# A hybrid decoder layer on one core: the output projection moved between the recurrence's steps, attention outputs with tokens as rows, and the low-rank work inside the first key slabs

## The reference, cut to what matters

```python
proj = x @ w_in[l]
y_rwkv = _rwkv7_mixer(proj[..., :RWKV_COLS], ...)
y_diff = _diff_attention(proj[..., RWKV_COLS:], ...)
mix = jnp.concatenate([y_rwkv, y_diff], axis=-1) @ w_out[l]
x = _layer_norm(DEEPNORM_ALPHA * x + mix, ln1_gain[l], ln1_bias[l])
h = jnp.square(jax.nn.relu(x @ w_ff1[l])) @ w_ff2[l]
x = _layer_norm(DEEPNORM_ALPHA * x + h, ln2_gain[l], ln2_bias[l])
...
# in the mixer: decay and a from low-rank products, kk = k * k_k normalised by head
w = -jax.nn.softplus(-(w0 + jnp.tanh(w_d) @ w_up)) - 0.5
a = jax.nn.sigmoid(a0 + a_d @ a_up);  g = jax.nn.sigmoid(g_d) @ g_up
y = (y - mean) * rsqrt(var + eps) * gn_gain + gn_bias;  out = (y + bonus) * g
...
# in the attention, for each head of 128 values
out = out * lax.rsqrt(jnp.square(out).mean(-1, keepdims=True) + SUBLN_EPS) * subln_gain
out = out * (1.0 - lambda_init)
```

## Time and profile before

| what | value |
|---|---|
| median of 3 runs | 1323.35 us (1322.83 to 1326.43) |
| the profiled execution | 1328.44 us, of which the span is 1326.7 us |
| PE busy | 1273.9 us (96%) |
| DVE, ACT, POOL busy | 738.2, 567.2, 82.3 us |
| mean granted TensorE clock | 0.986 |
| bytes read | 218.83 MB, 167 GB/s over the span |

### The profile page before, as it was taken

How to read it: one execution, slowest core, us unless ns; L and a number is a source line. 1 busy time by engine, 2 the same in 40 slices (tenths; PEclk the granted TensorE clock), 3 DMA queues, 4 the chain that set the end, 5 groups by cost and what they waited for, 6 DMA issues and landing times.

```text
span 1326.7 us, 24389 instructions
## 1 busy us (share of the span) xinstructions
PE 1273.9 (96%) x10200; PEld 1096.8 (83%) x10200; DVE 738.2 (56%) x762; ACT 567.2 (43%) x615; POOL 82.3 (6%) x53
## 2 busy tenths in 40 slices
PE   6999999999999889989999999999999999999995
PEld 6899999999777767877888888888888888888884
DVE  4367766363575135677555555555555555655557
ACT  4643444445554123454333333333344444444443
POOL 0021112000000010029200000000000000000000
PEclk9999999999999899999999999999999999999998
DMA  8254565223300234564555555555565555555541
GB/s 325 101 195 163 187 221 192 96 101 101 126 32 5 109 148 145 197 229 146 193 179 183 188 188 190 189 184 179 183 252 192 192 191 194 196 197 188 194 160 64
DMA packets 33671, 222.02 MB, mean 167 GB/s; under 512 B 4773, under 2 KB 5157, under 8 KB 7742
## 3 DMA queue, kind: packets, MB, share of 16 engines
q1 hardware_dynamic: 33598, 220.94, 47.2%
HBM read 218.83 MB, written 2.10 MB: 167 GB/s over the span
## 4 chain that ended last, share of the span: by engine, by line
PE 90%; DVE 5%; ACT 3%; issue 2%; DMA 0%; SPq 0%; DVEq 0%; ACTq 0%
PE ps L447 89%; DVE wlo L1362 1%; DVE x1f L1736 0%; DMA stage<-w_in 0%; ACT whi L1054 0%; DVE stats L1701 0%; DVE xres L1806 0%; PE ps L707 0%; DVE xres L1700 0%; DVE xres L1804 0%; ACT L1054 0%; DVE acts L1750 0%; ACT xres L1054 0%; ACT kr L1054 0%; DVE yt L1659 0%
## 5 line engine op out<-in xcount | busy, mean ns | idle before, releaser
L1362 DVE TENSOR_TENSOR wlo<-stage,whi 128x2048 fp32r<-128x2048 f32 x192 | 447.9, 2333 | 429.4 <-ACT whi L1054 428.3
L447 PE MATMUL ps<-acts,whi 128*128 128x256 f32 (+1 forms) x2400 | 622.8, 337 | 16.7 <-DVE wlo L1362 14.8
L1054 ACT ACTIVATE whi<-stage 128x2048 fp32r<-128x2048 f32 x194 | 371.8, 1917 | 593.5 <-PE ps L447 590.5
L447 PE MATMUL ps<-acts,wlo 128*128 128x256 f32 x1712 | 483.8, 283 | 0.5 <-issue 0.5
L447 PEld LDWEIGHTS ps<-acts,whi 128*128 128x128 f32 x2400 | 409.5, 191 | 72.9 <-issue 20.8
L447 PEld LDWEIGHTS ps<-acts,wlo 128*128 128x128 f32 x1712 | 327.2, 191 | 0.7 <-issue 0.7
L447 PE MATMUL ps<-whi,shi 128*128 128x512 f32 x632 | 249.5, 395 | 2.8 <-DVE slo L1673 2.7
L447 PE MATMUL ps<-wlo,shi 128*128 128x512 f32 x632 | 248.0, 392 | 0.0
L447 PE MATMUL ps<-whi,slo 128*128 128x512 f32 x632 | 247.8, 392 | 0.0
L447 PEld LDWEIGHTS ps<-whi,shi 128*128 128x128 f32 x632 | 119.5, 189 | 35.7 <-issue 6.8
L447 PEld LDWEIGHTS ps<-wlo,shi 128*128 128x128 f32 x632 | 119.5, 189 | 25.4
(11 more groups left out here) (206 smaller groups left out, 839.4 us busy)
## 6 DMA issues: line engine op xcount, KB each, us to landing
stage<-w_ff SPq DMA_DIRECT2D x128, 1024.0 KB, 4.9
stage<-w_in SPq DMA_DIRECT2D x51, 1024.0 KB, 4.9
stage<-w_out SPq DMA_DIRECT2D x16, 1024.0 KB, 4.9
xstage<-xT SPq DMA_DIRECT2D x4, 512.0 KB, 7.0
xres<-x SPq DMA_DIRECT2D x1, 2048.0 KB, 7.8
gain<-ln_gain SPq DMA_DIRECT2D x2, 1024.0 KB, 8.0
bias<-ln_bias SPq DMA_DIRECT2D x2, 1024.0 KB, 10.1
out<-xres SPq DMA_DIRECT2D x8, 256.0 KB, 2.2
```

Of the source, the lines that this page charges most:

```text
L447: return pe.matmul(out, lhsT, rhs, start=start, stop=stop, skip_group_check=True)
L1054: return act.activation(out, in_, func, **kw)
L1362: TTn(wlo[k0 % NHL][:, :], stage[k0 % NST][:, :], f(whi[k0 % NHL][:, :]), ALU.subtract).then_inc(s_lo, 1)
```

## The change

Six things are edited. (1) 18 products of a zeroed tile (`WARM`) stand ahead of slab 0, and slabs 0 to 2 are loaded and split in halves, with their columns in one layout of 384. (2) The low-rank block is cut into pieces that stand inside slabs 4 to 7 (`low_rank`); the sines move to chunks 6 to 8. (3) `bonus_and_kk(j - 1)` moves from c = 0 to c = 1, and the roots for it to c = 0; the triangular solves start one slab later. (4) The attention outputs are computed with tokens as rows, four heads at a time; the squares are summed by DVE, and PE transposes the normalised result (`heads_turned`). (5) The output projection goes by quarters of the columns (`out_rows`), and its first six slabs stand in pieces between the recurrence's steps and the group norm's; `w_out` is loaded earlier; the gate is copied out of PSUM by ACT. (6) The last slabs go by token tile, and the layer norm's additions by quarter, with `scales(0, 0)` behind the last of them.

```diff
+WARM = 18
...
-        FIRST_SLAB = (1, 8)
+        FIRST_SLAB = (2, 9)
...
+        def out_bank(a, q):
+            return (6, 4, 2, 0)[q] + a
...
+            def low_rank(g, part):
+
+                at_half = 2 * (g - G_MIX) + part
+                if at_half == 2:
+                    pe.wait_ge(s_cst, 16)
+                    pe.wait_ge(s_lup, 32)
+                    pe.wait_ge(s_lora, 1)
+                    pe.wait_ge(s_vec, 1)
+                    pe.wait_ge(s_free, 2)
+                    for a in range(TT_):
+                        for q in range(2):
+                            mm(ps[:, 4 + 2 * a + q, :], wt[:, tok(a)], wup[:, 512 * q:512 * q + 512]).then_inc(s_z, 1)
+                items = {3: range(0, 4), 4: range(4, 8), 5: (8, 9), 6: (10, 11), 7: (12, 13), 8: (14, 15)}
+                for n in items.get(at_half, ()):
+                    b, bk = n % NB, 4 + n % 4
+                    if n < 4:
+                        pe.wait_ge(s_sig, n + 1)
+                    else:
+                        pe.wait_ge(s_itemd, n - 3)
+                    if n < NB:
+                        mm(ps[:, bk, 0:S], aup[64:128, P * b:P * b + P], wa[64:128, :]).then_inc(s_item, 1)
+                    else:
+                        for a in range(TT_):
+                            last = mm(ps[:, bk, 256 * a:256 * a + 256], sig[:, a, P * b:P * b + P],
+                                      cst[:, C_SU:C_SU + 2 * P])
+                        last.then_inc(s_item, 1)
...
+            pe.wait_ge(s_zero, 1)
+            for _ in range(WARM):
+                mm(ps[:, 7, 0:2 * P], zeros[:, 0:P], zeros[:, P:3 * P])
...
+            def mix_values(i):
+
+                pe.wait_ge(s_atc, 4 * i + 4)
+                pe.wait_ge(s_vdc, 2 * i + 2)
+                if i == 0:
                     pe.wait_ge(s_smd, DH)
                 else:
-                    pe.wait_ge(s_osq, h - 1)
-                bank = mix_bank(h)
-                mm(ps[:, bank, 0:S], vd[:, 0, P * h:P * h + P], attT[h][:, 0:S], stop=False)
-                mm(ps[:, bank, P:S], vd[:, 1, P * h:P * h + P], attT[h][:, S:3 * P], start=False).then_inc(s_o, 1)
+                    pe.wait_ge(s_oc, 1)
+                for h in range(4 * i, 4 * i + 4):
+                    o, v = P * (h % 4), slice(P * h, P * h + P)
+                    mm(ps[:, 6, o:o + P], attT[h][:, 0:P], vd[:, 0, v])
+                    mm(ps[:, 7, o:o + P], attT[h][:, P:2 * P], vd[:, 0, v], stop=False)
+                    last = mm(ps[:, 7, o:o + P], attT[h][:, 2 * P:3 * P], vd[:, 1, v], start=False)
+                last.then_inc(s_o, 1)
...
-            def head_sums():
-
-                pe.wait_ge(s_osq, DH)
-                pe.wait_ge(s_sumw, 16)
-                for h in range(DH):
-                    last = mm(ps[0:DH, 6, 0:S], sumw[:, 37 - h:45 - h], osq[:, h, :], start=(h == 0), stop=(h == DH - 1))
-                last.then_inc(s_oss, 1)
-
-            def head_spread(p):
-
-                if p == 0:
-                    pe.wait_ge(s_sel8, 16)
-                    pe.wait_ge(s_ord, 1)
-                if p >= 2:
-                    pe.wait_ge(s_ydn, p - 1)
-                for j in range(2):
-                    last = mm(ps[:, 6 + p % 2, S * j:S * j + S], sel8[:, 2 * p + j, :], oinv[:, :])
-                last.then_inc(s_spr, 1)
...
+            def out_rows(g, kks, by_tile=False):
+
+                half, q, p = (g - G_OUT) // 8, (g - G_OUT) // 2 % 4, (g - G_OUT) % 2
+                w = g % NHL
+                if kks[0] == 0:
+                    halves_ready(g)
+                    pe.wait_ge(s_ohi[half], 2 * p + 2)
+                    pe.wait_ge(s_olo[half], 2 * p + 2)
+                order = [(kk, a) for kk in kks for a in range(TT_)]
+                if by_tile:
+                    order = [(kk, a) for a in range(TT_) for kk in kks]
+                for kk, a in order:
+                    blk, acc, cols = 4 * p + kk, ps[:, out_bank(a, q), :], slice(512 * kk, 512 * kk + 512)
+                    hi_, lo_ = oshi[half][:, blk, tok(a)], oslo[half][:, blk, tok(a)]
+                    end = half == 1 and p == 1 and kk == 3
+                    mm(acc, hi_, whi[w][:, cols], start=(half == 0 and blk == 0), stop=False)
+                    mm(acc, lo_, whi[w][:, cols], start=False, stop=False)
+                    last = mm(acc, hi_, wlo[w][:, cols], start=False, stop=end)
+                    if end and a == 0:
+                        last.then_inc(s_row, 1)
+                if kks[-1] == 3:
+                    last.then_inc(s_used, 1)
...
+            out_rows(G_OUT, (0, 1))
...
+            spread(0)
+            spread(1)
+            out_rows(G_OUT + 3, (1, 2, 3))
+            spread(2)
+            pe.wait_ge(s_gs, 4)
+            out_rows(G_OUT + 4, (0,))
+            spread(3)
+            out_rows(G_OUT + 4, (1, 2, 3))
+            out_rows(G_OUT + 5, range(4))
+            pe.wait_ge(s_gn, 7)
+            for g in range(G_OUT + 6, G_FF1):
+                out_rows(g, range(4), by_tile=(g - G_OUT) % 16 in (9, 11, 13, 15))
...
                 for c in range(3):
                     m = 3 * j + c
                     g, p0 = G_MIX + 2 * m, 2 * (m % 2)
-                    if c == 0 and j:
+                    if m == 6:
+                        angles()
+                    if c == 1 and j:
                         bonus_and_kk(j - 1)
                     if c == 1:
+                        if j == 0:
+                            dve.wait_ge(s_itemd, NB)
...
+            def head_sums(i):
+                dve.wait_ge(s_oc, i + 1)
+                for a in range(TT_):
+                    last = dve.tensor_reduce(osum[:, a, 4 * i:4 * i + 4], osq[a][:, :, :], AX_X, ALU.add)
+                last.then_inc(s_osum, 1)
+
+            def heads_normalised(i):
+                o = osum[:, :, 4 * i:4 * i + 4]
+                dve.wait_ge(s_osd, i + 1)
+                dve.reciprocal(o, o).then_inc(s_orc, 1)
+                dve.wait_ge(s_orc, i + 1)
+                for a in range(TT_):
+                    x = otok[:, a, 512 * i:512 * i + 512].rearrange("p (h q) -> p h q", h=4)
+                    last = TTn(x, x, osum[:, a, 4 * i:4 * i + 4].unsqueeze(2).broadcast_to([P, 4, P]), ALU.mult)
+                last.then_inc(s_on, 1)
...
+            lo(G_OUT + 4, G_OUT + 4)
             for g in range(4):
                 finished(g)
-            dve.wait_ge(s_lo, G_OUT + 1)
+                lo(G_OUT + 5 + g, G_OUT + 5 + g)
+                rwkv_lo(g)
...
-                kp = n % (KT // 2)
-                lo(G_OUT + n, G_OUT + n)
-                split(yt[:, 2 * kp:2 * kp + 2, :], n, n % 2, G_OUT + n - 1)
-                if n == 9:
-                    dve.wait_ge(s_xres, 16)
-                if 9 <= n < 13:
-                    add_and_measure(0, *FIRST_SWEEP[n - 9])
-            add_and_measure(0, 0, 2)
+            lo(G_OUT + 9, G_OUT + 9)
+            lo(G_OUT + 10, G_OUT + 10)
+            dve.wait_ge(s_xres, 16)
+            for q in range(3):
+                lo(G_OUT + 11 + 2 * q, G_OUT + 11 + 2 * q)
+                for a in range(TT_):
+                    add_and_measure(0, a, q)
+                if q < 2:
+                    lo(G_OUT + 12 + 2 * q, G_OUT + 12 + 2 * q)
             add_and_measure(0, 0, 3)
-            add_and_measure(0, 1, 2)
+            add_and_measure(0, 1, 3)
             scales(0, 0)
-            add_and_measure(0, 1, 3)
             scales(0, 1)
...
+            for g in range(G_OUT, G_OUT + 4):
+                slab(g, g, t["w_out"][g - G_OUT])
             sp.wait_ge(s_kb, 2)
             sp.dma_start(sel16[:, :, :], t["consts"][0:2 * NB, C_SEL:C_SEL + NB * P]
                          .rearrange("p (h q) -> p h q", q=P)).then_inc(s_sel16, 16)
             sp.dma_start(sumg[:, :], t["consts"][:, C_SUMW:C_SUMW + 32]).then_inc(s_sumg, 16)
-
+            for g in range(G_OUT + 4, G_OUT + 6):
+                slab(g, g, t["w_out"][g - G_OUT])
             sp.wait_ge(s_w, NC - 1)
             sp.dma_start(gup[:, :, :], t["g_up"]).then_inc(s_gup, 16)
-
-            sp.wait_ge(s_ydn, 4)
-            for g in range(G_OUT, G_OUT + 4):
+            sp.wait_ge(s_yp, 4)
+            sp.dma_start(xres[:, :, :], t["x"].rearrange("(a p) d -> p a d", p=P)).then_inc(s_xres, 16)
+            for g in range(G_OUT + 6, G_OUT + 8):
                 slab(g, g, t["w_out"][g - G_OUT])
-
-            sp.wait_ge(s_y, 4)
-            sp.dma_start(xres[:, :, :], t["x"].rearrange("(a p) d -> p a d", p=P)).then_inc(s_xres, 16)
-            slabs(G_OUT + 4, 0, KT // 4 - 1, t["w_out"][4:, :, :])
+            slabs(G_OUT + 8, 0, 2, t["w_out"][8:, :, :])
             slabs(G_FF1, 0, 1, t["w_ff1"])
```

More of the change, by code:

```diff
@@ L158, in build @@
         attT += [at("attT7", 22, [P, 3 * P])]
-        osq = at("osq", 2, [P, DH, S])
-        oinv = at("oinv", 3, [DH, S], byte=2048)
+        otok = at("otok", 23, [P, TT_, RW])
```

(36 more changed lines are left out.)

604 lines of the change are left out of this document (345 added, 259 removed).

## The result

The changed kernel takes 1339.3 us in the median of 4 runs (1334.5 to 1347.7) against 1323.5 before: a ratio of 1.013, with an interval of 1.009 to 1.017. It is slower by 16, where I had forecast 1321, and lies above the range. The profiled execution is one of 1342.1 with a span of 1340.2.

What follows compares the result with a forecast made beforehand. The prediction took PE, busy for 96% of the span, as the bound. Its terms, 1.6 - 0.8 - 1.7 - 3.8 + 8.6 - 1.4, made 2.5 us less: 1321 against the median of 1323.35, range 1305 to 1333.

Steps and rivals of the forecast that it cites:

- part 3: Mixing stage, `bonus_and_kk` at c = 1: `lo` comes late, PE waits 1.25 in each of three turns, 3.8 us lost.
- The rival with this cause: DVE blocked by POOL: `lo` waits for POOL's whole instruction, 3.3 instead of 1.25 in three turns; 1327 us, chance 0.03.
- the bound of 6.0: Upper bound of loss for `bonus_and_kk` at c = 1, if POOL stretches `lo` and the `ki` rows too.
- 1, the zeros, +1.6: Start: products of zeros raise PE's clock earlier, slab 2 ends at 29.7 instead of 31.34, 1.6 us gained.
- 2, slab 4, -0.8 and -1.7: Ahead of slab 4 PE waits 2.5 instead of 1.72, 0.8 lost; the lower clock behind it costs 1.7.
- 4, +8.6: Attention outputs to output projection's end: 6.7 less work, 1.8 more idle, 3.7 from the clock; 8.6 us gained.
- (a): Inside slab G_OUT + 4, `spread(3)` needs `finished(1)`, which stands behind a `lo` in DVE's order: PE waits 3.5.
- (b): Ahead of slab G_OUT + 6, which needs `finished(3)`, behind `lo(G_OUT + 7)`: PE waits 5.7.
- the issue gaps: PE's five unexplained gaps between attention outputs and output projection's end: 9.7 falls to 5.9 (bounds 2.7 and 9.7), 3.8 gained.
- The rival in which they vanish: PE's gaps without cause around the output projection vanish, another 4 of issue time: 1317 us, chance 0.14.
- 5, -1.4: Layer norm: `scales(0, 0)` ends 2.4 after the last product instead of 0.9, 1.4 us lost.
- My slower rival: Small products spread between slabs with waits bring 20 us more at the lower clock, 10 lost: 1331 us, chance 0.21.

Runs made afterwards that it cites:

- a_no_warm: The changed kernel without the 18 products of zeros (`WARM = 0`): 1346.7 us, ratio 1.017 to the kernel before.
- t_no_warm: The changed kernel with the orders of `bonus_and_kk`, `finished` and `scales(0, 0)` mended (1306.6), but without the products of zeros: 1309.5 us.
- a_scales_first: The changed kernel with `scales(0, 0)` ahead of the addition of tile 1's last quarter, nothing else: 1341.9 us, ratio 1.014.
- t_load: The changed kernel with `bonus_and_kk`, `finished` and `scales(0, 0)` orders mended (1306.6), plus slab 3's load ahead of the five small loads: 1307.1 us.
- t_order: The changed kernel with `bonus_and_kk`, `finished` and `scales(0, 0)` orders mended (1306.6), plus slab 4's two halves made ahead of the low-rank results: 1302.9 us.

## Why the prediction was wrong

The step that failed is part 3. It priced `bonus_and_kk` at c = 1 at 3.8, three waits of 1.25. Measured are three waits of 4.8, and a stretch at the lower clock behind each (0.51 from 110.5 to 117.3, in which PE is busy 4.1: some 2 lost each time). By the starts of `whi`, a turn of six slabs takes 43.2 (108.43 to 151.61) where it took 36.3, 6.9 more; the next one loses 7.5 and the third 7.7, 22.1 in all. Moving it behind `lo` gave back 19.1 in the medians. The step's own length of `bonus_and_kk`, 3.26, was right. It then took the `ki` group at its old length, 1.8, and beside POOL it takes 5.7; and it put the lower clock behind these waits at nothing.

I had the row for it, and read it wrongly. In the earlier trace rows `lo` at 91.68 took 2.77 and I put that down to running beside POOL's 3.35 of 92.26. But POOL's instruction takes 1.34 by itself (106.06 above). It was the one that waited, since `lo` had begun first. What held `lo` up is the POOL product ahead of that one, which I did not show, and at 97.44 it is POOL's last product:

```profile
91.01 1.30 POOL L1833 TENSOR_TENSOR bt<-bt,krv  x1 [90.56 <-DVE krv L1430]
...
97.03 1.29 POOL L1837 TENSOR_TENSOR ki<-ki,e  x1
```

The first ends at 92.31, 0.63 behind the start of `lo`, which is done 2.14 later. The second ends at 98.32, 0.88 behind the start of the `lo` of 3.04, done 2.16 later. Both `lo`s end some 2.15 behind POOL's instruction, close to their own 2.29, as if they had begun only there: the profile before held the evidence. The Trainium skill, "SBUF — State Buffer", section "SBUF: two separate sides", says just this: the shared ports are an exclusive lock between a GpSimd instruction and a DVE instruction with two SBUF inputs or in a two-port mode, whoever starts first holds them for the whole instruction, and the other blocks. I cited that rule against the trace, and as if `lo` had to be the one that waits; the runs agree with it (1.29 against 3.20 for POOL's product behind `lo`, 0.43 against 1.55 for DVE's row on `bt` beside POOL's). The rival with this cause had a chance of 0.03 and a time of 1327, because I priced it on `lo` alone, 3.3 a turn. It hit the three rows between as well, which stand right behind the instruction that releases POOL; the bound of 6.0, which names them, leaves 0.75 a turn for POOL.

The other terms, in order:

- **1, the zeros, +1.6.** They ended at 10.69, not 12.4, and slab 2 at 28.1, not 29.7: 3.2 gained, but hardly by the zeros. Without them (a_no_warm) slab 2 ends 0.3 later: with slabs 0 to 2 split in halves PE starts at 9.54 in place of 11.40, and runs at the lower clock for 3.7 (5.3 in t_no_warm) in place of 5.9. And slab 3's load landed at 25.05, so that PE waited 1.15 for its `wlo`. The work was there earlier than the loads. In the medians the zeros bring 3 (t_no_warm) and 7 (a_no_warm), most of it behind the start; both profiles without them have a wait of 2.8 or 2.4 ahead of slab 4 and the stretch behind it, a term that I did not have.
- **2, slab 4, -0.8 and -1.7.** Right in kind. The wait was 1.4 here, because slab 3 itself was late; the clock fell all the same for 6.8, which costs 3.4 (half of it, by the two levels). With slab 3 in time it is 2.4 to 2.8, as forecast at 2.5, and the stretch is 10.2 long, which costs 5.1 and not 1.7. Terms 1 and 2 make -0.9 together, and -1.4 was measured (slab 12): near by luck, since the gain and the loss were each larger.
- **4, +8.6.** Measured +12.7. Waits (a) and (b) came as worked out, 2.9 and 5.6 against 3.5 and 5.7, by the very instructions: `hi` 1.92, `lo` 2.29, `rwkv_lo` 0.60, the step 0.61. Taking them away brought 10.5. The term that was mis-sized is the issue gaps: 9.7 before, 2.0 after, where I took 5.9 and gave 2.7 as the bound. The rival in which they vanish was right and came together with the forecast. PE's busy time fell by 9.3, against 6.7 less work and 3.7 of clock in the forecast. That the loads of `w_out` made the gaps was only argued: no run moved the loads alone.
- **5, -1.4.** Measured -1.3, with the first `normalise` 2.4 behind the last product as worked out. But the lower clock from 602.0 to 608.8 has a share in it that the term did not have, and a_scales_first does not separate the two.

The terms as measured: the start -1.4 (at the end of slab 12), part 3 -22.1, part 4 +12.7, part 5 -1.3, together 12.1 slower. The spans differ by 13.5. Of the other 1.4, 1.1 are in PE's idle times in the first solve's slabs (1.03 and 0.51, ending at 242.80 and 255.95, against 0.46 ending at 235.23 before), a term that I had costed at nothing; the rest is not assigned. My slower rival had the wrong cause: the clock in 400 to 600 rose.

## What to carry to other kernels

Two engines that share a path must be costed as a pair: ask of each instruction that releases the other engine what stands behind it in its own queue, and price that at its own length plus the other's. A duration that is longer beside another engine says that one of the two waited; compare both with their length alone before deciding which. And a short wait is worth removing beyond its own length where it is followed by a lower clock. Where several waits stand in a row (load, then split), removing the first one hands its time to the last, as t_load shows; begin with the last one, as t_order does.
